# A three-layer fp32 transformer stack: the second norm's columns in another PSUM bank, an FFN unit loaded into a spare tile, the down weights' halves ahead of h, and copies and convolutions ahead of halves and table work

## Chip, cores and metric

One NeuronCore of a Trainium2 chip runs the whole program. The metric is the device time of one execution in microseconds.

## What is computed

Sequence 256, width 1024, fp32, batch 1. Two modulated layers and then one block of another kind:

```
cond = silu(c)
for l in 0, 1:
    sh_m, sc_m, g_m, sh_f, sc_f, g_f = split(cond @ ada_w[l] + ada_b[l], 6)
    h = x * (1 + sc_m) + sh_m
    y = even_mixer(h) if l == 0 else odd_mixer(h)
    x = layer_norm(ALPHA * x + (1 + g_m) * y)
    h = x * (1 + sc_f) + sh_f                       # the second norm's h
    u = causal_conv3(h @ ffn_w_up[l]);  y = (silu(gate(u)) * val(u)) @ ffn_w_down[l]
    x = layer_norm(ALPHA * x + (1 + g_f) * y)
even_mixer: DSA attention (8 heads, top-64 of scored keys, ALiBi) and a gated
            short convolution  yb = bg * conv3(cg * xb);  concat @ ev_w_out
odd_mixer:  multiscale pooling and MLA attention (8 heads, rope);  concat @ od_w_out
second block: h = rmsnorm(x); FOX (forgetting), MOBA and stick-breaking attention,
            gated sum of the three, @ w_out;  then  relu(h @ w_up)^2 @ w_down, rmsnorm
```

## The kernel before

Every product runs in three passes of reduced-precision operands: an operand is split into a high half (a copy rounded to fp32r) and a low half (the rest), and PE computes high x high, high x low and low x high. Weights come in units of up to 128 x 2048 elements (1 MB). For each unit g: SyncE loads it in two transfers into `raw[g % 2]` (`load_unit`); ACT writes the high half `uh` (`hi_unit`, line 839); POOL writes the low half `ul` (`lo_unit`, line 727); PE multiplies into bank 4 + g % 2. A load waits for the low half of the unit before it in its buffer, the high half waits until PE has used the one before it, PE waits for both halves. Units are numbered in order of use: G_CX[0..3] (pairs of columns for the short convolution), G_BG[0..1] (its gate), G_EO (out projection), FFN_G0[0].. (first FFN), and so on. The down weights of an FFN have a chain of their own: `raw_down`, `hi_down` (line 846), `lo_down` (line 733), tile `down`. The modulation tables `ada` are loaded in halves of 1 MB from ACT's and SyncE's queues and are summed on DVE (`modulation_half`, four operations at lines 1902 and 1903), spread between its other work.

Every engine's order of work is written out by hand; an engine does nothing out of order. PSUM banks are handed out by `turn(name, bank)`: a use of a bank may begin only when the use before it in the list is evacuated.

In an attention stage PE computes scores of a pair of heads, DVE subtracts the maximum and ACT takes the exponential, DVE scales (`normalize`), PE transposes, ACT copies (`evac_pt`, line 916), PE multiplies with v (`weighted`, lines 1537 and 1540), ACT and DVE take the result out in two halves (`out_high`, line 921; `out_low`, line 2083). Between these, PE multiplies the units of the next part in the portions of `FILL`; `DONE` says after which portion ACT handles a finished unit. In the DSA stage the fill is G_CX and G_BG; DVE's `convolution(b)` (lines 2309 to 2313) reads and frees the bank of G_CX[b], and `gate(i)` (lines 2325, 2327) that of G_BG[i]. The fifth unit, G_BG[0], goes to the buffer of the third, and its high half is made by `cg` for G_CX[2].

At the second norm of a layer DVE adds the last residual columns, takes statistics of both row blocks, POOL computes the powers (lines 739, 741), DVE normalises the two row blocks (line 2014, each raising `row_ready`), PE has meanwhile computed the modulation columns (`mod_columns`, line 1469) and transposes the rows (`transpose_rows`, line 1451), ACT makes h's high half (`h_high`, line 882), DVE the full h (`h_columns`, line 1959), POOL three quarters of the low half (`h_low`, line 766). `transpose_rows` claims all four banks of its turn before its first transpose. For layer 0 the columns use bank 2, also one of these four; for layer 1 bank 7. Then the FFN: first products (`first_units`, line 1408, and `second_unit`, line 1372), then the loop with `up` (48 products of 256 columns) and `downward` (12 of 512).

`layer_norm` (lines 1995 to 2008) is used once, behind the second layer's FFN; ACT squares its rows for the following rmsnorm (line 1187). Behind that come G_F and the units G_QKV[FOX]; ACT computes the forget gate's logarithm on 8 partitions at lines 1192 to 1194, with two table loads.

## Time and profile before

| | us |
|---|---|
| median of 3 runs | 1189.29 (1187.02 to 1191.23) |
| the profiled run | 1187.67 |
| its span, first to last instruction | 1185.9 |
| mean granted PE clock | 0.98 |
| PE busy | 1127.9 |
| POOL busy | 831.8 |
| ACT busy | 590.7 |
| DVE busy | 538.6 |
| read from HBM | 236.12 MB, 200 GB/s over the span |

The profile is one execution. A timeline row gives the start in us from the span's start, the length, engine, line and operation, and in brackets how long the engine was idle before it and what released it. Rows on SPq are DMA issues, not transfers. The page lists busy times; idle time of PE has to be found in the timeline.

### The profile page before, as it was taken

How to read it: one execution, taken by the hardware profiler on the slowest of the kernel's cores; microseconds unless marked ns; L12 is line 12 of the kernel's file. 1: busy time of each engine (PE TensorE's matmuls, PEld its weight loads, DVE VectorE, ACT ScalarE, POOL GpSimd, SP SyncE). 2: the span in 40 equal slices, each digit the busy share in tenths (PEclk: the TensorE clock that was granted, in tenths of full speed). 3: DMA queues.
4: the chain of work that ended last, by engine and by line, in shares of the span. 5: the costliest groups of instructions: out<-in, count | busy, mean ns of one | idle time of the engine just before them, and what ended most of it. 6: DMA issues, size and time to landing. Idle time of an engine off the chain costs nothing.

```text
span 1185.9 us, 21675 instructions
## 1 busy us (share of the span) xinstructions
PE 1127.9 (95%) x8119; PEld 1033.5 (87%) x8119; DVE 538.6 (45%) x1120; ACT 590.7 (50%) x894; POOL 831.8 (70%) x297
## 2 busy tenths in 40 slices
PE   6899898999999988999999989999999999999997
PEld 2799788999998987989999969999999988999996
DVE  4668677965657684594323350433111333111112
ACT  0445425545453554545545434555776544455444
POOL 3567467988876634798788737566656776988885
PEclk9899998999999999999999999999999999999999
DMA  9987587999987354597666415434444544766652
GB/s 341 323 270 199 201 276 242 342 330 320 320 276 248 114 143 147 176 288 240 183 188 181 138 36 177 139 112 142 143 143 143 185 153 127 211 186 187 192 178 88
DMA packets 253485, 238.03 MB, mean 201 GB/s; under 512 B 18076, under 2 KB 216529, under 8 KB 253425
## 3 DMA queue, kind: packets, MB, share of 16 engines
q1 hardware_dynamic: 235104, 198.70, 54.4%
q10 hardware_dynamic: 17712, 38.28, 9.0%
q8 instruction: 41, 0.67, 0.2%
q0 software_dynamic: 608, 0.22, 0.1%
q14 instruction: 20, 0.16, 0.0%
HBM read 236.12 MB, written 1.05 MB: 200 GB/s over the span
## 4 chain that ended last, share of the span: by engine, by line
PE 68%; DMA 7%; ACT 7%; DVE 7%; POOL 6%; issue 3%; SPq 0%; ACTq 0%; DVEq 0%; POOLq 0%
PE bank L1270 16%; PE bank L1271 16%; PE bank L1272 16%; POOL unit_lo L727 5%; ACT unit_hi L839 3%; DMA raw<-in_ev_w_in 3%; PE bank L1304 2%; PE bank L1295 2%; DMA raw<-in_ffn_w_up 2%; PE bank L1408 2%; PE bank L1296 2%; DMA ada<-in_ada_w 2%; PE bank L1331 1%; DVE x L2029 1%; PE bank L1324 1%
## 5 line engine op out<-in xcount | busy, mean ns | idle before, releaser
L727 POOL TENSOR_TENSOR unit_lo<-raw,unit_hi 128x2048 fp32r<-128x2048 f32 (+4 forms) x88 | 348.1, 3960 | 231.5 <-ACT unit_hi L839 230.6
L1270 PE MATMUL bank<-h_hi,unit_hi 128*128 128x256 f32 x1152 | 327.8, 285 | 2.9 <-POOL unit_lo L779 2.9
L1271 PE MATMUL bank<-h_lo,unit_hi 128*128 128x256 f32 x1152 | 326.6, 284 | 0.0
L1272 PE MATMUL bank<-h_hi,unit_lo 128*128 128x256 f32 x1152 | 326.6, 283 | 0.0
L779 POOL TENSOR_TENSOR unit_lo<-raw,unit_hi 128x2048 fp32r<-128x2048 f32 (+1 forms) x70 | 257.2, 3674 | 70.1 <-ACT unit_hi L986 65.2
L1270 PEld LDWEIGHTS bank<-h_hi,unit_hi 128*128 128x128 f32 x1152 | 221.5, 192 | 8.3 <-issue 5.5
L1271 PEld LDWEIGHTS bank<-h_lo,unit_hi 128*128 128x128 f32 x1152 | 221.5, 192 | 2.5
L1272 PEld LDWEIGHTS bank<-h_hi,unit_lo 128*128 128x128 f32 x1152 | 221.4, 192 | 0.0
L839 ACT ACTIVATE unit_hi<-raw 128x2048 fp32r<-128x2048 f32 (+4 forms) x98 | 163.1, 1666 | 103.4 <-DMA raw<-in_ffn_w_up 28.6
L782 POOL TENSOR_TENSOR down<-raw_down,down 128x1024 fp32r<-128x1024 f32 x70 | 176.5, 2522 | 0.0
L2160 DVE SCALAR_TENSOR_TENSOR work<-bank,cols,work 128x254 f32<-128x254 f32 (+1 forms) x176 | 72.6, 474 | 130.2 <-ACT work L973 130.2
L1270 PE MATMUL bank<-down,y_hi 128*128 128x512 f32 x296 | 116.5, 394 | 1.8 <-issue 0.9
L1271 PE MATMUL bank<-down,y_hi 128*128 128x512 f32 x296 | 116.0, 392 | 0.0
L1272 PE MATMUL bank<-down,y_lo 128*128 128x512 f32 x296 | 115.2, 389 | 0.0
L986 ACT ACTIVATE unit_hi<-raw 128x2048 fp32r<-128x2048 f32 (+1 forms) x60 | 90.8, 1514 | 5.1 <-DMA raw<-in_ffn_w_up 4.2
L971 ACT ACTIVATE work<-bank,cols 128x256 f32<-128x256 f32 x44 | 20.9, 474 | 118.2 <-PE bank L1272 105.2
L2189 DVE TENSOR_TENSOR bank<-bank,work 128x256 f32<-128x256 f32 x32 | 13.8, 433 | 135.3 <-ACT work L976 135.3
L1295 PE MATMUL bank<-h_hi,unit_hi 128*128 128x256 f32 x272 | 70.0, 294 | 2.5 <-DVE h_full L2313 2.5
L1012 ACT ACTIVATE down<-raw_down 128x1024 fp32r<-128x1024 f32 x60 | 63.3, 1056 | 14.5 <-PE bank L1272 14.4
L1296 PE MATMUL bank<-h_lo,unit_hi 128*128 128x256 f32 x272 | 68.5, 288 | 0.0
L1270 PEld LDWEIGHTS bank<-down,y_hi 128*128 128x128 f32 x296 | 55.8, 189 | 12.3 <-issue 1.9
L1272 PEld LDWEIGHTS bank<-down,y_lo 128*128 128x128 f32 x296 | 55.6, 188 | 12.1
(361 smaller groups left out, 2180.3 us busy)
## 6 DMA issues: line engine op xcount, KB each, us to landing
raw<-in_ffn_w_up SPq DMA_DIRECT2D x88, 512.0 KB, 5.2
raw<-in_w_in SPq DMA_DIRECT2D x60, 512.0 KB, 4.5
raw_down<-in_ffn_w_down SPq DMA_DIRECT2D x44, 512.0 KB, 5.5
ada<-in_ada_w ACTq DMA_DIRECT2D x16, 1024.0 KB, 6.9
raw<-in_w_up SPq DMA_DIRECT2D x64, 256.0 KB, 3.0
raw_down<-in_w_down SPq DMA_DIRECT2D x32, 512.0 KB, 3.5
...
```

The source lines that it names most:

```text
L727: nc.gpsimd.tensor_tensor(ul[g % 2][:, w], raw[g % 2][:, w], uh[g % 2][:, w].bitcast(F32), ALU.subtract).then_inc(lo_up, 1)
L779: nc.gpsimd.tensor_tensor(ul[s][:, 0:w], raw[s][:, 0:w], uh[s][:, 0:w].bitcast(F32), ALU.subtract).then_inc(lo_up, 1)
L782: nc.gpsimd.tensor_tensor(down[:, 1 - k, 1, :], rawd[1 - k][:, :], down[:, 1 - k, 0, :].bitcast(F32), ALU.subtract).then_inc(lo_dn, 1)
L839: nc.scalar.activation(uh[s][:, w], raw[s][:, w], ACT.Copy).then_inc(hi_up, 1)
L986: nc.scalar.activation(uh[s][:, 0:w], raw[s][:, 0:w], ACT.Copy).then_inc(hi_up, 1)
L1012: nc.scalar.activation(down[:, 1 - k, 0, :], rawd[1 - k][:, :], ACT.Copy).then_inc(hi_dn, 1)
L1270: nc.tensor.matmul(o, sh, mh, start=first, stop=False)
L1271: nc.tensor.matmul(o, sh, ml, start=False, stop=False)
L1272: return nc.tensor.matmul(o, sl, mh, start=False, stop=last)
L1295: nc.tensor.matmul(o[:, 0:S], uh[s][:, a], mh[:, kt, :], start=kt == 0, stop=False)
L1296: nc.tensor.matmul(o[:, 0:S], uh[s][:, a], ml[:, kt, :], start=False, stop=False)
L2160: return V.scalar_tensor_tensor(t[:, back:S], bank[4 + s][:, S * j:S * (j + 1) - back], w, t[:, back:S], ALU.mult, ALU.add)
```

## The change

- The turn of the first layer's second modulation columns goes from bank 2 to bank 6.
- The first unit of the first FFN is no longer loaded into `raw[g % 2]` but into `h_full` (`hff`), with a semaphore of its own, once both gate products (`bg_ready` 2) have read that tile; `h_columns(1)` waits for its low half before it writes there.
- The halves of each FFN's first down block are made before h instead of at the head of `ffn`: on ACT `hi_down` ahead of `h_high`, on POOL `lo_down` ahead of `h_low` behind a wait for `row_ready` (third FFN: behind the unit's low half).
- DSA attention: ACT makes the high half of G_BG[0] and issues a modulation load after the copies and `out_high` of the next pair; DVE runs convolutions 2 and 3 ahead of `out_low` and `normalize`.
- MLA attention: `hi_unit(G_OO[1])` one step later, behind the copies of heads 2 and 3.
- `layer_norm` handles one row block after the other.
- The copy of G_QKV[FOX][0], with the high half behind it, ahead of the forget gate's table work.

```diff
     def landing(g):
-        return g % 2 + 2 * (slot(g) > 0)
+        return 4 if g == FFN_G0[0] else g % 2 + 2 * (slot(g) > 0)
     ev_in, od_in, w2in = W["ev_w_in"][0], W["od_w_in"][0], W["w_in_2"][0]
...
         turn(("modr", 0, 0, half), half)
-    turn(("modc", 0, 1), 2)
+    turn(("modc", 0, 1), 6)
     turn(("last", 0), 3)
...
         bank_free = [sem(f"bank_free{i}") for i in range(8)]
-        raw_in = [sem(f"raw_in{i}") for i in range(4)]
+        raw_in = [sem(f"raw_in{i}") for i in range(5)]
         rawd_in = [sem(f"rawd_in{i}") for i in range(2)]
...
                    FOX: (o_h[1], o_l[1]), MOBA: (o_h[2], o_l[2]), "stick": (o_h[0], o_l[0])}
+        def raw_home(g):
+            return hff if g == FFN_G0[0] else raw[g % 2]
         def att_count(a, h):
...
         DONE[MLA][1] = [G_OO[0]]
-        DONE[MLA][2] = [G_OO[1]]
+        DONE[MLA][3] = [G_OO[1]]
...
                 u, s, at, landed = units[g], g % 2, slot(g), raw_in[landing(g)]
-                if before(g) >= 0:
+                if g == FFN_G0[0]:
+                    sp_.wait_ge(bg_ready, 2)
+                elif before(g) >= 0:
                     sp_.wait_ge(lo_up, before(g) + 1)
                 if u["kind"] == "pair":
-                    dst = raw[s][:, :].rearrange("p (t a n) -> p t a n", t=KD, a=2)
+                    dst = raw_home(g)[:, :].rearrange("p (t a n) -> p t a n", t=KD, a=2)
                     for a in range(2):
...
                 w = slice(slot(g), slot(g) + units[g]["width"])
-                nc.gpsimd.tensor_tensor(ul[g % 2][:, w], raw[g % 2][:, w], uh[g % 2][:, w].bitcast(F32),
+                nc.gpsimd.tensor_tensor(ul[g % 2][:, w], raw_home(g)[:, w], uh[g % 2][:, w].bitcast(F32),
                                         ALU.subtract).then_inc(lo_up, 1)
...
                 w = units[g0]["width"]
-                lo_down(d0)
                 def body(i, k):
...
             powers(("even",), spread, LN_EPS)
+            pool.wait_ge(row_ready, 2)
+            lo_down(FFN_D0[0])
             h_low(1)
...
             powers(("odd",), spread, LN_EPS)
+            pool.wait_ge(row_ready, 6)
+            lo_down(FFN_D0[1])
             h_low(3)
...
             lo_unit(G_WO[-1] + 2)
+            lo_down(FFN_D0[2])
             ffn(2)
...
                     act.wait_ge(bank_full[4 + s], before(g) // 2 + 1)
-                nc.scalar.activation(uh[s][:, w], raw[s][:, w], ACT.Copy).then_inc(hi_up, 1)
+                nc.scalar.activation(uh[s][:, w], raw_home(g)[:, w], ACT.Copy).then_inc(hi_up, 1)
             def hi_down(d):
...
                         out_high(a, p - 1)
+                    if p == 1 and a == DSA:
+                        hi_unit(G_BG[0])
+                        load_sum(SUM_ATT[2])
                     for g in DONE[a][2 * p + 1]:
...
                 act0 = sum(FFN_NB[:f])
-                hi_down(d0)
                 def body(i, k, fixed):
...
                     else:
-                        act.wait_ge(raw_in[s], i * 32 + (raw_need[g0 + k] + 32))
+                        act.wait_ge(raw_in[s], i * 32 + raw_need[g0 + 2 + k])
                         nc.scalar.activation(uh[s][:, 0:w], raw[s][:, 0:w], ACT.Copy).then_inc(hi_up, 1)
...
                 nc.scalar.activation(cgb[i % 2], b[:, 0:256], ACT.Copy).then_inc(cg_ready, 1)
-                hi_unit(g + 2)
+                if i != 2:
+                    hi_unit(g + 2)
             def gated(g):
...
                 act.dma_start(ada[a % 2].rearrange("p (t n) -> p t n", t=KD // 2), ada_half(a)).then_inc(ada_in[a % 2], 16)
-            AHEAD = {2: SUM_ATT[2], 3: SUM_ATT[3], 5: SUM_EVEN[0]}
+            AHEAD = {3: SUM_ATT[3], 5: SUM_EVEN[0]}
             def even_filler(g):
...
                     load_sum(SUM_EVEN[2])
+            hi_down(FFN_D0[0])
             h_high(1, ("modc", 0, 1), modT[:, 0, 24:32], modT[:, 0, 16:24])
...
                 other(g)
+            hi_down(FFN_D0[1])
             h_high(3, ("modc", 1, 1), modT[:, 1, 24:32], modT[:, 1, 16:24])
...
             hi_unit(G_F + 2)
+            evac_qkv(G_QKV[FOX][0], 0, 0)
             link(nc.scalar.activation(f_t[1], f_t[0], ACT.Abs))
             nc.scalar.activation(f_t[1], f_t[1], ACT.Ln, bias=1.0).then_inc(f_log, 1)
-            for j, g in enumerate(G_QKV[FOX]):
-                evac_qkv(g, 0, j)
+            for j, g in enumerate(G_QKV[FOX][1:]):
+                evac_qkv(g, 0, j + 1)
             attention(FOX, lambda g: evac_qkv(g, 1, g - G_QKV[MOBA][0]))
...
                 other(g)
+            hi_down(FFN_D0[2])
             h_high(5, "stage", mlp_gain, None)
...
             def h_columns(n, scale, shift):
+                if n == 1:
+                    dve.wait_ge(lo_up, FFN_G0[0] + 1)
                 def whole(q):
...
                     dve.wait_ge(var_ready, POWERS.index(name + (tt,)) + 1)
-                    ins = V.scalar_tensor_tensor(x[:, tt, :], x[:, tt, :], mv[:, tt, 0:1], lnrow[:, 0, :],
-                                                 ALU.subtract, ALU.mult)
-                    if tt < TT - 1:
-                        link.mark(ins)
-                    else:
-                        link(ins)
-                for tt in range(TT):
+                    link(V.scalar_tensor_tensor(x[:, tt, :], x[:, tt, :], mv[:, tt, 0:1], lnrow[:, 0, :],
+                                                ALU.subtract, ALU.mult))
                     powered(dve, name + (tt,))
...
                 for p in range(PAIRS):
+                    if middle and p:
+                        middle(p)
                     if p and a == DSA:
                         normalize(a, h)
-                    if middle:
+                    if middle and p == 0:
                         middle(p)
```

## Rows read from the trace of the kernel before

**Rows 1.** The page, part 1: busy time, share of the span and instructions of each engine.
```profile
PE 1127.9 (95%) x8119; PEld 1033.5 (87%) x8119; DVE 538.6 (45%) x1120; ACT 590.7 (50%) x894; POOL 831.8 (70%) x297
```

**Rows 2.** Waits of PE: who waited for whom, us in total, times, longest.
```profile
PE bank L1451 <- DVE x L2014: 4.7, 1, 4.7
```

**Rows 3.** Timeline of the DSA attention: start, us, engine, line, tiles, [idle before <- releaser].
```profile
119.36 1.91 ACT L839 ACTIVATE unit_hi<-raw 128x2048 fp32r<-128x2048 f32 x1 [1.39 <-DMA raw<-in_ev_w_in]
...
121.18 0.85 ACT L916 ACTIVATE work<-bank 128x384 f32<-128x384 f32 x2
...
122.33 0.42 DVE L2083 TENSOR_TENSOR y_lo<-bank,y_hi 128x256 fp32r<-128x256 f32 x1 [3.56 <-ACT y_hi L921]
...
122.91 0.65 PE L1537 MATMUL bank<-work,att 128*64 128x256 f32 x4 [1.84 <-DVE y_lo L2083]
...
129.17 2.34 DVE L1903 SCALAR_TENSOR_TENSOR bank<-att,cols,bank 128x512 f32<-128x512 f32 x3
...
137.37 0.36 PE L1295 MATMUL bank<-h_hi,unit_hi 128*128 128x256 f32 x1 [2.47 <-DVE h_full L2313]
...
150.99 0.39 PE L1324 MATMUL bank<-unit_hi,y_hi 128*128 128x256 f32 x1 [1.13 <-DVE y_lo L2083]
```

**Rows 4.** Windows: stretch, length, busy us of PE, PEld, DVE, ACT, POOL, PE clock, DMA share, GB/s.
```profile
121.00:125.00 4.00, 2.16 (x20) 1.54 (x20) 2.56 (x9) 1.30 (x4) 3.65 (x1) 1.00 0.83 295
...
137.50:142.00 4.50, 4.50 (x26) 4.50 (x27) 3.73 (x6) 2.40 (x2) 1.66 (x1) 0.62 0.67 229
...
225.00:250.00 25.00, 24.69 (x175) 23.13 (x175) 19.12 (x32) 12.98 (x18) 20.04 (x7) 1.00 1.06 344
...
452.80:458.00 5.20, 5.14 (x34) 3.53 (x35) 1.09 (x4) 0.38 (x2) 3.79 (x1) 0.71 0.59 194
```

**Rows 5.** Timeline of the first layer's second norm and the start of its FFN.
```profile
170.17 1.92 ACT L839 ACTIVATE unit_hi<-raw 128x2048 fp32r<-128x2048 f32 x1 [7.04 <-DMA raw<-in_ffn_w_up]
...
171.46 0.86 SPq L671 DMA_DIRECT2D raw_down<-in_ffn_w_down  x1
...
DMA to landing us min/median/max: 7.5/7.5/7.5
...
172.17 4.52 POOL L727 TENSOR_TENSOR unit_lo<-raw,unit_hi 128x2048 fp32r<-128x2048 f32 x1 [4.33 <-ACT unit_hi L839]
...
180.75 3.65 PE L1451 MATMUL bank<-consts,x 128*128 128x128 f32 x16 [4.67 <-DVE x L2014]
...
194.41 2.42 POOL L733 TENSOR_TENSOR down<-raw_down,down 128x1024 fp32r<-128x1024 f32 x1
...
201.51 0.38 PE L1270 MATMUL bank<-h_hi,unit_hi 128*128 128x256 f32 x1 [1.46 <-POOL unit_lo L779]
...
204.69 4.64 POOL L779 TENSOR_TENSOR unit_lo<-raw,unit_hi 128x2048 fp32r<-128x2048 f32 x1
...
210.11 0.28 PE L1270 MATMUL bank<-h_hi,unit_hi 128*128 128x256 f32 x1
```

**Rows 6.** Timeline, MLA attention and the start of the second layer's FFN.
```profile
450.10 1.91 ACT L839 ACTIVATE unit_hi<-raw 128x2048 fp32r<-128x2048 f32 x1
...
452.86 1.12 PE L1537 MATMUL bank<-work,att 128*64 128x256 f32 x4 [3.64 <-ACT work L916]
...
486.47 3.55 PE L1451 MATMUL bank<-consts,x 128*128 128x128 f32 x16
...
507.12 0.38 PE L1270 MATMUL bank<-h_hi,unit_hi 128*128 128x256 f32 x1 [1.45 <-POOL unit_lo L779]
```

**Rows 7.** Timeline, second block: first norm and the qkv units behind it.
```profile
694.40 3.38 PE L1451 MATMUL bank<-consts,att 128*128 128x128 f32 x16 [2.67 <-DVE att L2043]
...
717.94 1.48 PE L1304 MATMUL bank<-h_hi,unit_lo 128*128 128x256 f32 x8 [1.92 <-POOL unit_lo L727]
...
719.13 4.57 POOL L727 TENSOR_TENSOR unit_lo<-raw,unit_hi 128x2048 fp32r<-128x2048 f32 x1 [1.25 <-ACT unit_hi L839]
...
725.27 1.12 PE L1304 MATMUL bank<-h_hi,unit_lo 128*128 128x256 f32 x8
```

## Prediction

> **What bounds the kernel now.** I read the page first: PE is busy in 95% of the span, POOL in 70%, ACT in 50% and DVE in 45% [rows 1]. No other engine is near PE over the whole, so a change that takes no matmul away can only win PE's idle time. The table of PE's waits names the largest places; one of them is 4.7 us for DVE's normalised rows [rows 2]. I then laid PE's timeline end to end and listed every hole above a quarter of a microsecond: some 48 us in 27 places, of which 15 us lie before the first layer's projections and cannot be touched by this change. Six holes lie where the diff works: 1.84 and 2.47 us in the DSA attention [rows 3], 4.67 and 1.46 us around the first FFN's start [rows 5], 3.64 us in MLA [rows 6], 1.45 us at the second FFN's start [rows 6]; two smaller ones, 2.67 and 1.92 us, stand in the second block [rows 7]. A hole can cost more than itself: behind the 2.47 us hole the granted clock is 0.62 of full over the next 4.5 us, and behind the 3.64 us hole 0.71 over 5.2 us, that is, part of each stretch at 1.2 instead of 2.4 GHz; behind the 1.84 us hole it stays 1.00 [rows 4].
>
> All times below are in the profiled run: span 1185.9 us, run 1187.67 us, 1.6 us (0.14%) under the median of 1189.29. I sum against 1187.67 and add the 1.6 at the end.
>
> **DSA attention, first hole.** ACT converts G_BG[0] (1.91 us, begun at 119.36 after 1.39 us of waiting for its load) ahead of the copies of heads 2 and 3, which start at 121.18; out_high(0) and DVE's out_low(0) at 122.33 follow, and PE starts at 122.91 [rows 3]. With the copies first, they start when their transposes are there (about 118.2), end 0.85 later, out_high(0) ends near 119.5, and the conversion starts then: 0.1 us later than now, since its load lands at 119.36 anyway. It cuts nothing: the half is first read near 126. DVE now does convolution(2) ahead of out_low(0). It is free of its modulation sum at 118.8, a convolution takes 1.9 us (four operations, 0.42 + 0.48 + 1.00), so out_low(0) ends near 121.1 and PE, which comes free at 121.07, waits about 0.2 instead of 1.84. **Gain 1.6.** If the convolution were to wait, the whole 1.84 would stay.
>
> **Second hole.** PE waits at 137.37 for convolution(3), which frees the bank of the last pair unit [rows 3]. Now DVE does out_low(1), four scalings (1.8 us) and only then the convolution, ending at 137.2. In the new order convolution(2) is out of the way before scores of heads 6 and 7 arrive, so the softmax pieces run about 3 us earlier, the modulation sum (3.1 us, its last three parts at 129.17 [rows 3]) ends near 128.5, and convolution(3) follows at once and ends near 130.4, against PE's need near 133.1. **Gain 2.5, and 1.7 more for the clock**: the 24 matmuls behind the hole take 4.6 us, 0.12 us each at full clock would be 2.9. What is late next is out_low(3): the ACT conversion of the second out-projection unit and a 3.1 us modulation sum stand before it, so the 1.13 us hole at 150.99 [rows 3] grows to about 1.35. Attention sum: 1.6 + 2.5 + 1.7 - 0.2 = **5.6 us**, bounds 3.5 (clock gain absent, conversion late) and 6.2.
>
> **The first layer's second norm.** Today the first FFN unit's load waits until a raw buffer is free, lands at 170.17, ACT had idled 7.04 us for it, and its low half keeps POOL from 172.17 to 176.69; only then come the powers of the norm, though DVE's statistics of the first rows are ready at 173.7. PE has its columns done at 176.08 and begins the transposes at 180.75 [rows 5]. With the load in h_full, released by the second gate product (near 140), it is issued right behind the last out-projection unit and lands some 6 us before ACT can use it. ACT converts it when the third out-projection unit is done, POOL ends its low half about 0.8 us after the last unit, before the first statistics. Its powers then run 2.9 us earlier. The columns' bank was the bank of a transpose; all four transposes' banks are claimed before the first one, so PE had to wait for DVE's column additions behind both rows. In bank 6 the first eight transposes start with the first row block. The second layer's norm is already built so: transposes start at 486.47, without a hole, 3.6 us after its last out-projection unit [rows 6]. I take that pattern: **4.7 us**. DVE's new wait for the low half, ahead of h_full, finds it done; behind it nothing is held.
>
> **The halves of the first down block.** hi_down (1.06 us) moves ahead of h_high. In the first layer its load, issued at 171.46, lands 7.5 us later at 179.0 [rows 5], after the time at which ACT would want it in the new order (177.9 in today's times). The pieces in front of it in the queue shrink by the one unit that has gone ahead, so I expect 177 to 178; the hold on ACT is 0 to 2.2 us and I take 0.3. POOL's lo_down, 2.42 us [rows 5], moves from behind the second FFN unit into the idle time between powers and h_low; that removes the 1.46 us hole at 201.51 [rows 5] and the 1.45 us hole at 507.12 [rows 6]. But the block after it is next: its low half ends at 209.33 (204.69 + 4.64) and PE takes it at 210.11 [rows 5]. That half hangs on a load that starts when the second unit's low half is done, which does not move. So of 1.46 only the slack of 0.8 is won, and in the second layer 0.5. In the third FFN POOL is not late; 0. Sum of the norm and the halves of layer one: 4.7 - 0.3 + 0.8 = **5.2 us**, bounds 2.8 and 7.0 (PE's first products at full clock); layer two **0.5**, bounds -0.5 and 1.6.
>
> **MLA.** hi_unit(G_OO[1]), 1.91 us from 450.10, stands ahead of the copies on which PE waits until 452.86 [rows 6]. Behind them, it leaves a hole of 1.8. The half is used a whole attention later; its raw buffer comes free 0.9 us later, the load behind that has over 10 us to spare. **1.8 us, and 0.8 for the clock** (1.6 is lost behind the hole now, and a hole of 1.84 left the clock full, one of 1.92 at 717.94 did not: its eight matmuls take 1.48 where 1.12 is usual [rows 4, 7]). Sum **2.6**, bounds 1.0 and 3.4.
>
> **Second block.** layer_norm in row order finishes no sooner (four operations of 1.2 to 1.3 us in both, two more exposed waits, +0.1), but ACT squares the first rows during it, so the first transposes start 0.9 earlier; the last rows do not. Of the hole of 2.67 [rows 7] I take **0.7**, bounds -0.2 and 1.6. Moving the copy of the first qkv unit and the conversion behind it ahead of two table loads brings the low half of unit two 1.4 us forward; its hole of 1.92 shrinks to 0.5 and its slow clock goes. Then unit three is the bound: its low half, 719.13 + 4.57 = 723.70, hangs on a load that this edit leaves in place, while PE takes it at 725.27 [rows 7]. So at most 1.5; the units behind alternate between load, half and low half in about 12 us for a pair against 11.5 of PE, which takes part of it back: **0.8**, bounds 0 and 1.5. The forget-gate table work, now later, is needed four units on.
>
> **Sum.** 5.6 + 5.2 + 2.6 + 0.5 + 0.7 + 0.8 = 15.4. 1187.7 - 15.4 = 1172.3; plus 1.6: **1173.9 us**.
>
> **Rivals.** (A) The lead is lost in the first FFN. From 225 to 250 the DMA engines' share is 1.06 at 344 GB/s [rows 4], and each 8.5 us block moves 2.6 MB. If its loads cannot come earlier, the 10.8 us won in front of it go and 4.6 stay: 1184.7. For it: the saturation. Against: PE had almost no hole there, and most loads are released by halves that come earlier too. The Trainium skill (DMA: Bandwidth & Descriptors, Issuing engines are not separate DMA queues) says that transfers of all issuing engines interleave on the same 16 DMA engines, so the early unit competes with ACT's table loads; by that this rival's time is the one to expect. Chance 0.13. (B) ACT is held in hi_down because the down load does not move: 2.2 us in layer one, and the pushed-back POOL chain loses the 0.8: 1173.9 + 2.7 = 1176.6, 0.14. (C) The freed holes bring the clock more than counted and all upper bounds fall together: about 1168, 0.12. (D) The edits don't reach: the holes are taken over by the next wait in each place and only the columns' bank works (2 us or less): 1187, 0.06. (E) Slower: the FFN's raw buffer becomes the bound. Two blocks pass one buffer in 17 us (8.6 from one up product at 201.51 to the next at 210.11 [rows 5]); if the displaced loads fall into a rhythm in which each cycle takes longer than 18.5, ten cycles cost more than 15.4. Priced at 19.0 that is 20 us: 1194. Against it: nothing in the loop's order changes. 0.05.
>
> **Numbers.** Forecast 0.50. About 0.3% (3.6 us) is what a measurement can tell. Faster: 0.50 + 0.12 + 0.14 + 0.09 of (A) = 0.85; same: 0.04 of (A) and 0.06 = 0.10; slower 0.05. The range 1168.0 to 1183.0 takes in the bounds of the terms, (B), most of (C) and the milder half of (A).
>
> **What would show it.** Right: no hole above 0.5 us before the weighted products of DSA pairs 1 and 2, and clock 1.00 there; transposes straight behind the columns near 170; lo_down between powers and h_low; MLA's hole near 1.8. Wrong: ACT's hi_down starting after the transposes end; holes before the up products of the first FFN; PE idle for `unit_lo` in qkv unit three beyond 2 us. I am wrong as a whole if the first FFN's loop starts less than 8 us earlier than now.

## The result, and the profile after

| | before | after |
|---|---|---|
| median of 6 runs | 1189.97 us (1187.02 to 1193.26) | 1177.47 us (1173.04 to 1180.54) |
| profiled run | 1187.67 | 1176.84 |
| its span | 1185.9 | 1175.0 |
| mean granted clock | 0.98 | 0.985 |

The ratio of the medians is 0.9893, 95% interval 0.9877 to 0.991: the kernel is 12.5 us faster. The forecast was 1173.9 with a range of 1168.0 to 1183.0. Of the 3.6 us between forecast and result 2.9 are the gain (15.4 forecast); the other 0.7 is the median of the kernel before, 1189.97 over six runs for the 1189.29 over three that the forecast started from. The two profiled spans differ by 10.9 us.

The page's first part, which answers to [rows 1] (busy us, share of the span, instructions):

```profile
PE 1126.1 (96%) x8119; PEld 1030.3 (88%) x8119; DVE 539.2 (46%) x1120; ACT 590.9 (50%) x894; POOL 832.3 (71%) x297
```

All engines do the same work; the 10.9 us came out of PE's idle time and of time in which its clock was low. Line numbers have moved: the products are now 1287 to 1289 and 1312 to 1313, transposes 1468, columns 1486, `hi_unit` 849, `hi_down` 856, `lo_unit` 733, `lo_down` 739, `evac_pt` 926.

The attention, against [rows 3]: ACT's copies, conversion, DVE's out_low, and PE's weighted products of pairs 1 and 2, from the timeline of the kernel after:

```profile
118.50 0.87 ACT L926 ACTIVATE work<-bank 128x384 f32<-128x384 f32 x2
...
120.37 1.92 ACT L849 ACTIVATE unit_hi<-raw 128x2048 fp32r<-128x2048 f32 x1 [0.72 <-DMA raw<-in_ev_w_in]
...
121.18 0.41 DVE L2098 TENSOR_TENSOR y_lo<-bank,y_hi 128x256 fp32r<-128x256 f32 x1
...
121.74 0.65 PE L1554 MATMUL bank<-work,att 128*64 128x256 f32 x4
...
132.85 0.65 PE L1554 MATMUL bank<-work,att 128*64 128x256 f32 x4
...
145.81 0.39 PE L1341 MATMUL bank<-unit_hi,y_hi 128*128 128x256 f32 x1 [1.12 <-DVE y_lo L2098]
```

Neither weighted product has a bracket: PE no longer waits there. Only the hole before the out projection is left, 1.12 us as it was.

The first layer's second norm, against [rows 5]:

```profile
167.27 4.69 PE L1486 MATMUL bank<-consts,accg 128*128 128x1 f32 x32
...
169.91 1.91 ACT L849 ACTIVATE unit_hi<-raw 128x2048 fp32r<-128x2048 f32 x1 [6.20 <-DMA raw<-in_ffn_w_up]
...
171.82 3.65 PE L1468 MATMUL bank<-consts,x 128*128 128x128 f32 x16
...
173.87 1.06 ACT L856 ACTIVATE down<-raw_down 128x1024 fp32r<-128x1024 f32 x1 [2.05 <-DMA raw_down<-in_ffn_w_down]
...
175.53 0.55 PE L1425 MATMUL bank<-h_hi,unit_hi 128*128 128x256 f32 x1
```

The 4.67 us hole is gone: the transposes run straight behind the column products. But these took 4.69 us where the kernel before needed 3.6 (172.45 to 176.08): the clock fell under them, as the windows of the kernel after show (stretch, its length, PE busy, PEld busy, the other engines, granted clock, DMA share, GB/s):

```profile
167.20:169.60 2.40, 2.40 (x24) 2.40 (x23) 2.23 (x7) 0.00 (x0) 2.00 (x3) 1.00 1.11 343
169.60:171.90 2.30, 2.30 (x13) 2.30 (x13) 1.51 (x4) 1.91 (x1) 1.21 (x2) 0.50 1.04 394
```

And ACT waited 2.05 us for the down block's load in `hi_down`. Both cost PE less than they show, because they overlap: h was not wanted before the slow transposes were through. What the later halves still cost here is a hole of 0.73 us for POOL's `h_low`, which now stands behind `lo_down`:

```profile
181.70 1.22 PE L1425 MATMUL bank<-h_lo,unit_hi 128*128 128x256 f32 x8 [0.73 <-POOL h_lo L772]
```

The second layer's norm holds what I had not forecast. Three of DVE's five column operations of 128x8, POOL's low half and PE's first product of the kernel after:

```profile
478.02 2.35 POOL L739 TENSOR_TENSOR down<-raw_down,down 128x1024 fp32r<-128x1024 f32 x1 [0.93 <-DVE x L2029]
...
478.18 0.17 DVE L1943 TENSOR_TENSOR cols<-bank,cols 128x8 f32<-128x8 f32 x1
478.26 2.13 DVE L1949 TENSOR_TENSOR small<-cols 128x8 f32<-128x8 f32 x1
480.43 0.17 DVE L1950 TENSOR_TENSOR cols<-cols 128x8 f32<-128x8 f32 x1
...
481.42 0.36 PE L1425 MATMUL bank<-h_hi,unit_hi 128*128 128x256 f32 x1 [1.01 <-ACT h_hi L892]
```

An operation that takes 0.16 us in the kernel before took 2.13, to 0.02 us behind the end of POOL's instruction. The columns were late, so h was, and PE had a new hole of 1.01 us.

By stage, from the starts of PE's blocks in the traces (us; the last column is the gain):

| stretch | before | after | gain |
|---|---|---|---|
| DSA attention: pair 0's weighted products to the norm's columns | 62.57 | 56.80 | 5.8 |
| first layer: the norm's columns to the next norm's columns | 204.17 | 201.10 | 3.1 |
| there to the second unit of layer two (clock only) | 16.75 | 18.43 | -1.7 |
| MLA: pair 0's weighted products to the norm's columns | 37.90 | 34.70 | 3.2 |
| layer two: transposes to the end of the FFN's products | 195.66 | 196.48 | -0.8 |
| layer_norm: to the transposes | 12.27 | 11.90 | 0.4 |
| qkv units: second unit to FOX's first weighted products | 52.25 | 52.13 | 0.1 |

These sum to 10.1. The rest of the 10.9 is starts (-0.6) and the third FFN's start, where the clock was 0.79 in the kernel before and 1.00 in the kernel after over the 7 to 8 us at the first products (+1.5), and small pieces. The numbers below are such differences of starts too.

One trace is one execution, and the traces of all 14 kernels show how far a stretch moves by itself. Without the edits of its stage, the first stretch takes 61.98 to 63.42 us (five kernels), with them 56.79 to 56.88 (seven): that gain is far outside the spread. The third stretch takes 16.7 us in seven kernels, 18.4 in six and 15.9 in one, with and without the edits, so its -1.7 is chance; so is the third FFN's +1.5. Layer two's stretch takes 194.91 to 196.87 us in the seven kernels whose layer two is that of the kernel before, so its -0.8 cannot be told from nothing.

### The profile page after: what moved, and what is told of

The parts are those of the page before. It is cut to its first block, busy times and chain, and to the rows that moved or that the text cites. A ratio compares the mean times of both kernels' runs of the same rounds, so it can differ in the third digit from the quotient of the medians.

```text
span 1175.0 us, 21678 instructions
## 1 busy us (share of the span) xinstructions
PE 1126.1 (96%) x8119; PEld 1030.3 (88%) x8119; DVE 539.2 (46%) x1120; ACT 590.9 (50%) x894; POOL 832.3 (71%) x297
## 3 DMA queue, kind: packets, MB, share of 16 engines
HBM read 236.12 MB, written 1.05 MB: 202 GB/s over the span
## 4 chain that ended last, share of the span: by engine, by line
PE 71%; DMA 8%; POOL 6%; ACT 6%; DVE 5%; issue 3%; SPq 1%; ACTq 0%; POOLq 0%; DVEq 0%
PE bank L1287 17%; PE bank L1288 17%; PE bank L1289 17%; POOL unit_lo L733 5%; PE bank L1312 3%; PE bank L1321 3%; PE bank L1313 2%; ACT unit_hi L849 2%; DMA raw<-in_ffn_w_up 2%; PE bank L1425 2%; DMA ada<-in_ada_w 1%; PE bank L1528 1%; PE bank L1348 1%; DMA raw<-in_ev_w_in 1%; DVE x L2044 1%
## 5 line engine op out<-in xcount | busy, mean ns | idle before, releaser
L733 POOL TENSOR_TENSOR unit_lo<-raw,unit_hi 128x2048 fp32r<-128x2048 f32 (+5 forms) x87 | 343.7, 3955 | 220.0 <-ACT unit_hi L849 219.2
L849 ACT ACTIVATE unit_hi<-raw 128x2048 fp32r<-128x2048 f32 (+5 forms) x97 | 161.3, 1664 | 103.5 <-DMA raw<-in_ffn_w_up 27.3
```

Source lines behind the costliest of these rows:

```text
L733: nc.gpsimd.tensor_tensor(ul[g % 2][:, w], raw_home(g)[:, w], uh[g % 2][:, w].bitcast(F32), ALU.subtract).then_inc(lo_up, 1)
L849: nc.scalar.activation(uh[s][:, w], raw_home(g)[:, w], ACT.Copy).then_inc(hi_up, 1)
```

## Experiments

### The attention's two halves

dsa_act is the kernel before with ACT's half, dsa_dve with DVE's:

```diff
# dsa_act
+                    if p == 1 and a == DSA:
+                        hi_unit(G_BG[0])
+                        load_sum(SUM_ATT[2])
...
-                hi_unit(g + 2)
+                if i != 2:
+                    hi_unit(g + 2)
# dsa_dve
                 for p in range(PAIRS):
+                    if middle and p:
+                        middle(p)
                     if p and a == DSA:
                         out_low(a, p - 1)
...
-                    if middle:
+                    if middle and p == 0:
                         middle(p)
```

> The kernel before with ACT's half of the DSA edit alone: the high half of G_BG[0] and the table load behind the copies and out_high of the next pair; DVE's order stays. The forecast gave the attention 5.6 us for both halves. Theory 1, the first hole (1.84 us before the weighted products of pair 1) is ACT's alone: the copies of heads 2 and 3 start 1.9 us earlier, DVE's out_low(0) stands ahead of normalize and convolution in the old order and comes at once, so the hole is gone; the second hole (2.47 us, PE waiting for convolution 3) is DVE's order: the softmax and the scalings still stand ahead of the convolution, and the hole stays at 2 to 2.5 us. From the start of the weighted products of pair 0 to the first product behind the attention's last hole: 1.6 to 1.8 us less than in the kernel before. Theory 2, the two are coupled: both holes stay or both go.

> The kernel before with DVE's half of the DSA edit alone: convolutions 2 and 3 ahead of out_low and normalize; ACT's order stays. Theory 1, the second hole is DVE's: convolution 3 ends before PE needs the bank, the 2.47 us hole is gone and with it the slow clock behind it (0.62 over 4.5 us, 1.7 us), 4.2 us together; the first hole stays at 1.84, since ACT's copies come as late as before. Theory 2: convolution 2 now stands in DVE's way of out_low(0), whose input comes 1.9 us later than in the kernel after, and the first hole stays or grows by up to 0.2. Theory 3: without ACT's half the convolution waits for cg of G_CX[2], and the second hole stays.

Measured: from pair 0 to the columns 58.10 us with ACT's half and 60.49 with DVE's, against 62.57 without and 56.80 with both. ACT's half alone brings 4.5, DVE's alone 2.1, both 5.8. In time, dsa_act is 1187.05 us, ratio to the kernel before 0.9969 (0.9949 to 0.9988), and dsa_dve 1186.94, ratio 0.9976 (0.9963 to 0.999): 3.7 and 2.9 us. The places, PE's rows of dsa_act and then of dsa_dve:

```profile
135.18 0.35 PE L1299 MATMUL bank<-h_hi,unit_hi 128*128 128x256 f32 x1 [1.39 <-DVE h_full L2317]
```

```profile
123.97 1.01 PE L1537 MATMUL bank<-work,att 128*64 128x256 f32 x4 [2.22 <-DVE y_lo L2083]
```

With ACT's half the first hole is gone and the second falls from 2.47 to 1.39, and the clock behind it is 1.00, where behind 2.47 it was 0.62 [rows 4]. So the second hole was partly made by the first, through the pieces that ran later, and the slow clock behind it goes with either edit. With DVE's half alone the second hole is gone, but the first grows to 2.22, and now the clock falls there: 0.63 over the 4.6 us behind it, in the windows of dsa_dve:

```profile
118.00:121.70 3.70, 3.70 (x33) 3.55 (x31) 3.22 (x6) 1.66 (x2) 0.00 (x0) 1.00 0.95 298
123.90:128.50 4.60, 4.53 (x27) 3.33 (x28) 3.03 (x11) 0.29 (x2) 3.02 (x1) 0.63 0.29 106
```

Theory 1 of dsa_act had the places right and the price wrong (1.6 to 1.8 expected, 4.5 measured). In dsa_dve theory 1 holds for the second hole; the first grew by 0.4, but not for theory 2's reason: DVE had done its convolution and stood idle 2.04 us for ACT's copy, which stood behind a conversion that began at 120.43, 1.1 later than in the kernel before (0.4 against the start of pair 0), since its load landed later. That is no effect of the edit: in the five kernels without either half the first hole is 1.84 to 2.60 us. In the three of them where it is 2.30, 2.43 and 2.60, the clock falls behind it and the second hole is 1.39 or 1.40, at full clock; where it is 1.84 and 2.05, the second is 2.47 with the slow clock behind it. So without the edits a slow clock stood behind one of the two holes in every trace, and not always the same one.

### The norm: bank and load

```diff
# bank_only
-    turn(("modc", 0, 1), 2)
+    turn(("modc", 0, 1), 6)
# load_only
+                if g == FFN_G0[0]:
+                    sp_.wait_ge(bg_ready, 2)
-                if before(g) >= 0:
+                elif before(g) >= 0:
...
+                if n == 1:
+                    dve.wait_ge(lo_up, FFN_G0[0] + 1)
```

> The kernel before with one edit: the first layer's second modulation columns in bank 6 instead of bank 2. The forecast gave the norm 4.7 us for bank and early load together and did not split them. Theory 1, both are gates in a row: POOL's powers still wait for the low half of the first FFN unit (end 176.69), the first rows are normalised at 178.5, and the transposes begin there instead of at 180.75: 2.2 us earlier, and the hole of 4.67 shrinks to about 2.4. In time 2 us faster than the kernel before. Theory 2, the bank does nothing without the load: 0. Theory 3, the bank is the whole gate: 4.7 us.

> The kernel before with one edit: the first FFN's first unit loaded into h_full, released by the second gate product. Theory 1: powers and normalised rows come about 2.9 us earlier, but the transposes still wait for bank 2, which DVE frees behind both row blocks and behind PE's last column product (176.1 plus 0.9): they start near 177.2 instead of 180.75, 3.5 us earlier, the hole shrinks from 4.67 to about 1.1 us. The sum of this and of the bank alone (2.2) is more than 4.7, since both cut the same hole. Theory 2: the load is no help, because ACT's high half and POOL's low half of the unit are still in front of the powers: less than 1 us. Theory 3: the unit's early transfer pushes the loads behind it (the table for the column sums, the second FFN unit) later, and the columns' products start later than 172.4: the gain shrinks by as much. In time 3 us faster than the kernel before.

Measured: ratios to the kernel before 0.9975 (0.996 to 0.999) and 0.9969 (0.9954 to 0.9985), 3 and 3.7 us. From the columns' start to the transposes' start 6.31 and 5.97 us, against 8.30: 2.0 and 2.3 each, and with both edits 8.30 - 3.57 = 4.7 (halves_back, below). PE's rows of bank_only and of load_only:

```profile
180.58 3.65 PE L1451 MATMUL bank<-consts,x 128*128 128x128 f32 x16 [2.69 <-DVE x L2014]
```

```profile
179.69 3.65 PE L1457 MATMUL bank<-consts,x 128*128 128x128 f32 x16 [2.11 <-DVE x L2023]
```

By the clock time of the row bank_only looks no faster than the kernel before (180.75), because in this execution its columns began 1.8 us later, at 174.27; those of load_only began at 173.72. As bank_only has no early load, the late start does not show theory 3 of load_only.

Theory 1 holds for the bank (2.4 expected, 2.69 left). For the load it holds in kind, not in size: 1.1 us of hole expected, 2.11 left. Each edit takes away half of the hole of 4.67 us, and together all of it.

### Where the halves stand

halves_back puts them at the head of the FFN again, pool_cols changes what POOL waits for, both from the kernel after:

```diff
# halves_back
-            hi_down(FFN_D0[0])
             h_high(1, ("modc", 0, 1), modT[:, 0, 24:32], modT[:, 0, 16:24])
...
                 act0 = sum(FFN_NB[:f])
+                hi_down(d0)
...
-            pool.wait_ge(row_ready, 2)
-            lo_down(FFN_D0[0])
             h_low(1)
# pool_cols
-            pool.wait_ge(row_ready, 2)
+            evacuated(pool, ("modc", 0, 1))
             lo_down(FFN_D0[0])
...
-            pool.wait_ge(row_ready, 6)
+            evacuated(pool, ("modc", 1, 1))
             lo_down(FFN_D0[1])
```

> The kernel after, with the high and low halves of each FFN's first down block put back at the head of the FFN; all other edits stay. Theory 1: ahead of h the low half costs what it wins. In layer two's norm of the kernel after, POOL's low half (2.35 us from 478.02) runs beside DVE's 128x8 fold of the columns, which takes 2.13 instead of 0.16 us, and PE loses 1.4 us before the first products; by the fourth up block the 1.5 us won at the third is gone as well. So here: fold at 0.17 us, no hole before the first products of the second FFN, the hole before the third up block back at some 1.4 us in both FFNs, and from the transposes to the seventh up block 55.2 to 55.5 us in both (55.9 and 56.0 in the kernel after, 55.5 and 55.2 in the kernel before). In time 0.5 to 1.5 us faster than the kernel after, near 1176.5. Theory 2, the prediction's terms: the halves are worth 0.8 and 0.5 us, so this kernel is 1.3 us slower than the kernel after, near 1178.8, and the distances from the transposes to the seventh up block do not shrink.

> The kernel after, with one wait changed: POOL begins the low half of the first down block of FFN one and two only when DVE has finished the modulation columns, instead of when the rows are normalised. Theory 1 (POOL's low half holds DVE's small two-operand operations): in layer two the fold is back at 0.17 us, ACT's first h_high follows the first full bank at about 478.8 instead of 480.7, the hole of 1.02 us before the first products is gone and they start 1.4 us earlier, at about 4.6 instead of 5.6 us or more after the transposes' start (4.60 in the kernel after, 3.20 in the kernel before); in layer one nothing moves, since there POOL waits for the high half anyway. Theory 2 (the fold was late for another reason: a semaphore or the order of DVE's queue): it keeps 2 us and the hole stays. How much of the 1.4 reaches the end: all of it, 1176.1, if nothing in the second FFN's loop is tighter than PE; none, 1177.5, if the loads of the third and fourth up blocks bound it.

Measured: 1176.95 us, ratio 0.9898 (0.9869 to 0.9927), and 1176.15, ratio 0.9868 (0.9844 to 0.9893); neither can be told from the kernel after by time. In the traces, layer two: from the transposes to the second unit 9.83 and 9.73 us, against 11.35 in the kernel after and 10.12 in the kernel before. POOL and DVE of pool_cols at that place:

```profile
479.99 0.16 DVE L1949 TENSOR_TENSOR small<-cols 128x8 f32<-128x8 f32 x1
...
480.50 2.37 POOL L739 TENSOR_TENSOR down<-raw_down,down 128x1024 fp32r<-128x1024 f32 x1 [1.69 <-DVE cols L1951]
```

The fold (L1949) takes 0.16 us again once POOL's instruction starts behind it; it was the overlap that held it. That settles theory 1 on the fold. In halves_back it takes 0.16 as well. To the end of the FFN's products nothing can be told: 195.19 with the halves ahead of h (pool_cols) and 195.45 with them at the head of the FFN (halves_back), against 194.91 to 196.87 in the seven kernels with layer two as before.

In layer one the other wait of pool_cols changes nothing, since POOL waits longer for ACT's `hi_down` in both kernels (3.66 and 4.25 us). Its column products ran at full clock, and so it shows what the slow ones had covered in the kernel after:

```profile
174.66 1.06 ACT L856 ACTIVATE down<-raw_down 128x1024 fp32r<-128x1024 f32 x1 [2.07 <-DMA raw_down<-in_ffn_w_down]
...
176.31 0.55 PE L1425 MATMUL bank<-h_hi,unit_hi 128*128 128x256 f32 x1 [1.82 <-ACT h_hi L892]
```

and its windows behind that hole:

```profile
176.30:181.00 4.70, 4.69 (x22) 4.70 (x23) 4.04 (x7) 3.17 (x7) 4.70 (x4) 0.50 0.43 168
181.00:184.70 3.70, 3.70 (x28) 3.70 (x28) 0.25 (x1) 0.00 (x0) 3.70 (x2) 0.85 0.71 265
```

From the columns to the second unit: 17.17 us in pool_cols, 15.49 in the kernel after, 13.64 in halves_back, 18.53 in the kernel before. So bank and load alone bring 4.9, and with ACT held in `hi_down` 1.4 to 3.0 of it are left. Of halves_back's expectation the fold, the missing hole and the time came true, and layer two took 55.0 us to the seventh up block (55.2 to 55.5 expected). Layer one took 56.8, because its loop lost part of what the norm had gained. Pool_cols went by its theory 1.

### Taking the hold away, and the loop behind it

down_early is pool_cols with the down load ahead of the two FFN units; mix puts layer one's halves behind h and keeps layer two's ahead; downs_early loads a second down block early:

```diff
# down_early
+            sp_.dma_start(rawd[0][:, :], FFN_DOWN[0][0:P, :]).then_inc(rawd_in[0], 16)
             for k in range(2):
                 load_unit(FFN_G0[0] + k)
...
             for j, g in enumerate(G_EO):
+                if g == G_EO[-1]:
+                    hi_down(FFN_D0[0])
                 other(g)
-            hi_down(FFN_D0[0])
             h_high(1, ("modc", 0, 1), modT[:, 0, 24:32], modT[:, 0, 16:24])
# downs_early
+            for k in range(2):
+                sp_.dma_start(rawd[k][:, :], FFN_DOWN[0][k * P:(k + 1) * P, :]).then_inc(rawd_in[k], 16)
# mix
             h_high(1, ("modc", 0, 1), modT[:, 0, 24:32], modT[:, 0, 16:24])
+            hi_down(FFN_D0[0])
             load_rows(0, W["ln_mix_g"][0:1, :], W["ln_mix_b"][0:1, :])
...
             lo_unit(G_EO[-1] + 2)
+            lo_down(FFN_D0[0])
             ffn(0)
```

> The kernel of pool_cols (the kernel after, with POOL's low half of the first down block behind the modulation columns) and two edits more in layer one: the first down block is loaded ahead of the two first FFN units instead of behind them and a table half, and ACT makes its high half before it waits for the last out-projection unit, in time in which it was idle. Theory 1, rival B of the prediction at its full price: in pool_cols ACT waits for the down load (2.07 us) with h_high queued behind it, PE stands 1.83 us and then runs slowly, and from the columns to the second FFN unit it takes 17.2 us against 13.6 in halves_back. Here that wait is gone: 13.6 us again, no hole behind the transposes, no hole of 1.45 us before the third block either, and the time is some 3 us below pool_cols: 1173. Theory 2, the first FFN's loads take it back: the modulation table halves and the blocks' loads have no room (the DMA engines' share is 0.9 to 1.1 from 190 to 250), DVE waits for a table half with PE's product behind it as in halves_back, and more than 2 us are lost again by the eighth block: 1175 to 1176. Theory 3, the down load pushes the two FFN units later and the transposes wait for the powers: 1177 or more.

> down_early with the second down block of the first FFN loaded early as well, right behind the first one, when the DMA engines have room (their share is 0.55 from 160 to 167 in the kernel after); the loads inside the loop then start with the third block. It moves 0.52 MB more out of the saturated stretch, some 1.6 us at 320 GB/s. Theory 1 (the loads bound the first blocks of the loop): the loss beyond the beat of 8.5 us falls from 4.3 by 1 to 1.6 us, and the time to 1173.5 to 1174.2. Theory 2 (latency and order, not volume): no change, 1175.2. Theory 3: the block pushed ahead of the two units delays them, and the columns-to-second-unit distance grows past 14.5 us.

> The kernel after with the halves of the first down block where each layer bears them: in layer one behind h_high and h_low as in the kernel before (so ACT is not held by the down load), in layer two ahead of them with POOL's low half behind the modulation columns (so DVE's fold is not held), in the third FFN as in the kernel after. Theory 1: layer one runs as in halves_back, 13.6 us from the columns to the second FFN unit and 201.2 to 201.7 to the next columns, layer two as in pool_cols, 9.7 us from the transposes to the second unit and 195.2 us to the end of the FFN's products; together 0.3 us faster than halves_back and 1.5 to 2 us faster than the kernel after, 1175.5 to 1176. Theory 2: the halves' place is worth nothing in either layer, because the loop's loads set the pace behind it: 1177.5, as after.

To see whether traffic sets the loop's pace, the table halves in the first FFN were cut to a quarter, in the kernel before and in down_early:

```diff
+                            part = slice(0, 1) if f == 0 else slice(0, KD // 2)
...
+                                          src[:, part, :]).then_inc(ada_in[1 - k], 16)
```

> The kernel before, but the modulation table halves that are loaded inside the first FFN bring only the first quarter of their rows (0.26 MB instead of 1.05 MB a block; the sums on DVE run as before over what lies there, so the second layer's modulation is not the reference's). It takes away traffic of the first FFN and nothing else; it is the base for down_early_light. In the kernel before PE loses 2.4 us there beyond its beat of 8.5 us a block (1.8 at the second block, for POOL's low half of the down block; 0.5 and 0.1 later, for DVE behind a table half). Theory 1: the 1.8 stays, the 0.6 goes; from the columns of the second norm to the columns of the next norm 203.6 us instead of 204.2. Theory 2, the loads are no bound in the kernel before: no change.

> down_early with the same lighter table halves in the first FFN (a quarter of the rows; the second layer's modulation is not the reference's). Question: where did the gain of the first layer's second norm go? From the columns to the second FFN unit down_early is 4.1 us shorter than the kernel before (14.5 against 18.5), halves_back 4.9; but to the next norm's columns only 2.1 and 2.5, since both lose 4.3 to 4.6 us in the first FFN's loop beyond the beat of 8.5 us, where the kernel before loses 2.4. Theory 1, the loads bound the loop (rival A of the prediction in part): with three quarters of the table traffic gone DVE no longer waits 4.6 us for a table half at 232.9 nor ACT 5.4 us for the unit at 194.8, the loss beyond the beat falls from 4.3 to below 1, and from columns to columns it is 199 us or less, 4.5 to 5.5 us shorter than before_light. Theory 2, the loss comes from the order of ACT's and DVE's work, whatever the traffic: it stays at 4, and the difference to before_light stays near 2.

Both light kernels leave out three quarters of the rows of those table halves, so they are no candidates, only probes. The steady blocks of the loop take 8.5 us each; what lies beyond that, from the start of the first down block to that of the nineteenth, is its loss. All kernels with something different in layer one (us), and the two with one half of the attention's edits, whose layer one is that of the kernel before:

| | columns to second unit | loss in the loop | columns to next columns |
|---|---|---|---|
| before | 18.53 | 2.3 | 204.17 |
| before_light | 18.61 | 2.3 | 204.24 |
| bank_only | 16.54 | 2.3 | 202.16 |
| load_only | 16.22 | 2.6 | 202.10 |
| after | 15.49 | 2.3 | 201.10 |
| pool_cols | 17.17 | 2.2 | 202.72 |
| halves_back | 13.64 | 4.5 | 201.65 |
| mix | 13.64 | 2.7 | 199.67 |
| down_early | 14.48 | 4.2 | 202.04 |
| downs_early | 16.27 | 3.6 | 203.21 |
| down_early_light | 14.54 | 1.3 | 199.17 |
| dsa_act | 18.54 | 3.9 | 205.79 |
| dsa_dve | 18.48 | 2.8 | 204.60 |

Times: down_early 1175.16 (ratio 0.9874, 0.9853 to 0.9896), downs_early 1177.68 (0.989, 0.987 to 0.991), mix 1176.35 (0.9884, 0.9863 to 0.9906), before_light 1188.66 (0.9988, 0.997 to 1.0005), down_early_light 1171.85 (0.9846, 0.982 to 0.9873, two runs). The hold is gone in down_early (no hole behind the transposes), but the loop then loses 4.2 us, and the time is theory 2's 1175 to 1176. Three of its holes, with the table half that DVE waited for and the unit that ACT waited for:

```profile
194.79 1.92 ACT L851 ACTIVATE unit_hi<-raw 128x2048 fp32r<-128x2048 f32 x1 [5.36 <-DMA raw<-in_ffn_w_up]
...
198.57 0.47 PE L1290 MATMUL bank<-down,y_hi 128*128 128x512 f32 x1 [1.43 <-DVE y_lo L2212]
...
225.37 0.47 PE L1290 MATMUL bank<-down,y_hi 128*128 128x512 f32 x1 [0.85 <-DVE y_lo L2212]
...
232.88 0.76 DVE L1923 SCALAR_TENSOR_TENSOR bank<-ada,cols,bank 128x512 f32<-128x512 f32 x1 [4.64 <-DMA ada<-in_ada_w]
...
235.10 0.47 PE L1290 MATMUL bank<-down,y_hi 128*128 128x512 f32 x1 [0.99 <-DVE y_lo L2212]
```

With three quarters of the table traffic gone, the holes at 198.57 and 235.10 are gone, the loss is 1.3, and the stretch is 5.1 us shorter than before_light, where down_early was 2.1 shorter than the kernel before. The lighter tables alone change nothing in the kernel before. So theory 1 of down_early_light holds but for a fraction (199.17 for "199 or less", a loss of 1.3 for "below 1"): three quarters of the table halves' traffic cost down_early's loop 2.9 us, and the kernel before nothing. The hole of 0.85 at 225.37 stays, and is not the table halves' traffic.

The same shows where nobody touched layer one. In dsa_act PE reaches the second unit 3.7 us earlier than in the kernel before, and the loop loses 3.9 instead of 2.3. DVE waits there for a table half, and PE for DVE behind it; a hole of 1.05 us for DVE follows a block later.

```profile
219.27 0.76 DVE L1907 SCALAR_TENSOR_TENSOR bank<-ada,cols,bank 128x512 f32<-128x512 f32 x1 [2.65 <-DMA ada<-in_ada_w]
...
221.49 0.47 PE L1274 MATMUL bank<-down,y_hi 128*128 128x512 f32 x1 [0.65 <-DVE y_lo L2196]
```

A caution on the size: halves_back and mix are the same program in layer one, and their loops lost 4.5 and 2.7, though mix came earliest of all (second unit at 180.33). That is 2 us of run against run, about what the loop takes back, so an early PE is not enough by itself. The light pair's 2.9 is larger than it, with one trace each, but the order of halves_back, down_early and pool_cols in this table is not settled. mix was expected at 201.2 to 201.7 and came to 199.67, yet its median is no better than the others'.

downs_early went by theory 3: its two down blocks push the first FFN unit back, ACT waits 6.63 us for it and the powers stand behind its low half:

```profile
165.72 1.92 ACT L856 ACTIVATE unit_hi<-h_full 128x2048 fp32r<-128x2048 f32 x1 [6.63 <-DMA h_full<-in_ffn_w_up]
```

```profile
174.23 3.65 PE L1476 MATMUL bank<-consts,x 128*128 128x128 f32 x16 [2.37 <-DVE x L2037]
```

### The three edits elsewhere

```diff
-        DONE[MLA][2] = [G_OO[1]]
+        DONE[MLA][3] = [G_OO[1]]
...
             hi_unit(G_F + 2)
+            evac_qkv(G_QKV[FOX][0], 0, 0)
             link(nc.scalar.activation(f_t[1], f_t[0], ACT.Abs))
...
-                for tt in range(TT):
                     powered(dve, name + (tt,))
                     V.scalar_tensor_tensor(x[:, tt, :], x[:, tt, :], rstd[:, tt:tt + 1], lnrow[:, 1, :],
```

All three are made in the kernel before.

> The kernel before with the three edits that lie elsewhere: MLA's hi_unit(G_OO[1]) one step later, layer_norm in row order, the copy of G_QKV[FOX][0] ahead of the gate's tables. They lie in stretches of their own and are read one by one. MLA, theory 1: the hole of 3.64 falls to 1.85 us and the slow clock behind it goes in part, 2.6 to 3.2 us from the weighted products of pair 0 to the columns of the second norm. Layer_norm, theory 1: the hole ahead of the transposes falls from 2.67 to 2.3 us, that is 0.4, and not the 0.7 of the forecast, since the last rows come no sooner. The copy, theory 1: the hole of 1.92 falls to 0.46 and the slow stretch behind it goes, but the third and a later qkv unit have holes of 1.2 and 1.1 us that the kernel before does not show: 0.8 or less is left of 2. Theory 2 for the copy: those later holes are the run's and not the edit's, and the whole 2 us stays. All in all 3.5 to 4.5 us faster than the kernel before.

Measured: 1183.15 us, ratio 0.9946 (0.9926 to 0.9965), by its interval 4.2 to 8.8 us. The parts in the trace are MLA 37.90 - 34.71 = 3.2, layer_norm 12.27 - 11.89 = 0.4 and the copy 52.25 - 50.75 = 1.5, together 5.1. Between the last two, from the transposes to the second qkv unit, rest_only is 0.5 slower than the kernel before, which leaves 4.6 of the 5.1. For MLA theory 1 holds in full, for layer_norm as far as the transposes' start. The copy's later holes are the edit's: they stand in the kernel after and in rest_only alike (1.21 and 1.10 us; 1.21 and 1.21). The kernel after:

```profile
707.16 1.21 PE L1321 MATMUL bank<-h_hi,unit_lo 128*128 128x256 f32 x8 [0.46 <-POOL unit_lo L733]
...
714.38 1.21 PE L1321 MATMUL bank<-h_hi,unit_lo 128*128 128x256 f32 x8 [1.21 <-POOL unit_lo L733]
...
727.25 1.21 PE L1348 MATMUL bank<-unit_lo,h_hi 128*128 128x256 f32 x8 [1.10 <-POOL unit_lo L733]
```

Yet 1.5 us stay, where the profiled kernel after kept 0.1. The difference is a drop of the clock some 12 us ahead of FOX's weighted products, at work that has no hole. In before, bank_only and load_only the clock there is 0.66 over 5 us, and in all six kernels without the copy the stretch takes 52.2 to 52.3. Of those with the copy, it is 1.00 in rest_only, pool_cols, halves_back, down_early and mix (stretch 50.5 to 50.8) and 0.66 to 0.68 in after, downs_early and down_early_light (52.1 to 52.4). The kernel after and pool_cols, windows of 3 us:

```profile
734.00:737.00 3.00, 3.00 (x19) 2.27 (x20) 3.00 (x11) 2.97 (x9) 2.64 (x1) 0.87 0.82 283
737.00:740.00 3.00, 3.00 (x17) 3.00 (x17) 2.93 (x11) 2.08 (x10) 1.90 (x1) 0.56 0.03 4
```

```profile
735.00:738.00 3.00, 3.00 (x22) 2.28 (x23) 3.00 (x11) 2.97 (x10) 2.75 (x1) 1.00 0.78 272
738.00:741.00 3.00, 3.00 (x27) 3.00 (x27) 2.93 (x11) 2.03 (x10) 1.80 (x1) 1.00 0.04 6
```

## Why the prediction came out as it did

**DSA attention, 5.6: right, 5.8.** From pair 0 to pair 1, with the first hole, 13.03 - 11.27 = 1.8 (1.6 forecast); from pair 2 to pair 3, with the second and its clock, 11.39 - 7.39 = 4.0 (2.5 + 1.7). What I called two edits for two holes is coupled: ACT's half alone brings 4.5 of the 5.8, and the clock behind the second hole is full where that hole is 1.39. Against the spread of the kernels without the edits (61.98 to 63.42) the gain is 5.2 to 6.6. The hole before the out projection did not grow, so the 0.2 taken off for it was not needed.

**Second norm and halves of layer one, 5.2: 3.1, and 1.5 in pool_cols.** The term of 4.7 for bank and load was right (4.9 in halves_back and mix, to the second unit). Two sizes were wrong. "The hold on ACT is 0 to 2.2 us and I take 0.3": it is 2.05 and 2.07. The down load's issue came 5.3 us earlier (171.46 to 166.18), as did the whole stage, while the transposes came 8.9 earlier; its landing, 7.7 us behind the issue, was no earlier for the unit that had gone ahead. This is rival B: against halves_back the stretch to the second unit lost 3.5 in pool_cols, where the clock stayed low behind the hole as well, and 1.9 in the kernel after, where 1.0 lies ahead of the transposes (the slow column products) and 0.9 behind them (the hole of 0.73 for `h_low` most of it). And "the slack of 0.8 is won": the hole of 1.46 is gone, but the loop's loss is 2.3 as before. Two holes behind it took back what it had brought. In the kernel after:

```profile
194.25 1.92 ACT L849 ACTIVATE unit_hi<-raw 128x2048 fp32r<-128x2048 f32 x1 [4.39 <-DMA raw<-in_ffn_w_up]
...
198.03 0.47 PE L1287 MATMUL bank<-down,y_hi 128*128 128x512 f32 x1 [0.44 <-DVE y_lo L2209]
...
212.14 4.61 POOL L784 TENSOR_TENSOR unit_lo<-raw,unit_hi 128x2048 fp32r<-128x2048 f32 x1
...
215.09 2.74 DVE L2044 TENSOR_TENSOR x<-x,att 128x1024 f32<-128x1024 f32 x1
...
224.86 0.47 PE L1287 MATMUL bank<-down,y_hi 128*128 128x512 f32 x1 [0.87 <-DVE y_lo L2209]
```

and the same addition in the kernel before, where the hole in this place is 0.31:

```profile
220.59 4.63 POOL L779 TENSOR_TENSOR unit_lo<-raw,unit_hi 128x2048 fp32r<-128x2048 f32 x1
...
224.56 1.74 DVE L2029 TENSOR_TENSOR x<-x,att 128x1024 f32<-128x1024 f32 x1
```

Only the smaller hole, 0.44, stands behind a load, and that is all of rival A that the kernel after shows. The larger has the size that it keeps in down_early_light (0.84), and DVE works in front of it from 211.65 without a wait. One piece of that work is 1.0 us longer than before: the addition ends 1.08 us behind the end of the POOL instruction beside it in both kernels, as if it were held until then, and more of POOL's is left when it starts. That it is the hold of the small fold again, and that it makes the hole, is argued from these rows; no run changed it alone. The gain at the second unit, 8.2 us, is 8.3 at the next norm's columns, so A at its full price is refuted.

**Halves of layer two, 0.5: -0.8, inside the spread.** The step that failed is the plan itself: I took POOL's time between powers and h_low for idle and free, and did not ask what DVE does in it. What it cost is certain as far as the second unit: 11.35 us from the transposes, against 9.72 to 10.25 in the thirteen other kernels. How much of that reaches the FFN's end is not: the kernel after's 196.48 lies inside the 194.91 to 196.87 of the kernels without the edit, and so does what the term is worth with the collision removed (195.19 in pool_cols).

The Trainium skill (SBUF — State Buffer, Who interferes with whom, and SBUF: two separate sides) says that a DVE instruction with two SBUF inputs contends with a GpSimd one that reads SBUF, and that whoever starts first keeps the shared ports for its whole instruction. By that rule, the trace agrees: L1949 has both inputs in `cols`, started 0.24 us behind POOL's, and ended with it; L1943, with one input in PSUM, ran in 0.17 beside it. The prediction had not weighed it.

**MLA, 2.6: 3.2.** The hole fell to 1.84 as forecast:

```profile
444.50 0.65 PE L1554 MATMUL bank<-work,att 128*64 128x256 f32 x4 [1.84 <-ACT work L926]
```

and the clock returned in full, 1.4 instead of 0.8. This stretch can be worth more: it takes 37.9 to 38.0 us in three kernels without the edit, 40.4 to 40.5 in three others, and 34.7 in all eight with it. By the mean of the six the edit brings 4.5, and that the profiled kernel before was one of the faster three is chance.

**layer_norm, 0.7: 0.4.** The hole is 2.29 for 2.67. The first rows' gain of 0.9 was not a gain, since the stage ends with the last rows: in seven of the eight kernels with the edit PE stands again, for 0.47 us, between the two row blocks' transposes (0.34 or less without it). Behind it little or nothing is left. From the FFN's end to the second qkv unit six of the eight take 25.2 to 25.3 us, and five of the six without the edit 25.1 to 25.5.

**FOX copy, 0.8: 0.1 in the profiled run, 0.1 and -0.2 in two others, 1.5 to 1.7 in five.** Unit three did become the bound (1.21 us), as written, but I had not priced the clock behind. The mean of the eight is 1.0, so the 0.8 is near, by luck in part.

**Sum.** With the clock in its more frequent state for the copy, the terms are 5.8 + 3.1 + 3.2 - 0.8 + 0.4 + 1.5 = 13.2, near the 12.5 of the medians and 2.2 under my 15.4. Against the forecast's terms: the attention 0.2 more, MLA 0.6 more and the copy 0.7 more; layer one 2.1 less, layer two's halves 1.3 less, layer_norm 0.3 less. The errors half cancel, and the range held the result with rival B come true and little of A. Two of these sizes are soft: MLA would be 4.5 by the mean, and layer_norm and the copy together bring 1.3 to 1.6 and not 1.9 from the FFN's end to FOX in the same five kernels. That the sum lands within 1 us of the medians is therefore no proof of its parts. My general test (the loop at least 8 us earlier) was met: the second unit is 8.2 earlier. "ACT's hi_down starting after the transposes end" would have shown rival B in pool_cols (174.66 against 174.48), and missed it in the kernel after (173.87 against 175.47).

What stays open: why the clock falls at column products and ahead of FOX in some executions and not in others, how much of the 2 us between equal loops is the DMA's chance, and what the layer-two halves bring once they no longer collide.
